# Seven products in place of eight in the MLP's second matrix, for 24 of its 32 row tiles

## The chip, the cores and the metric

One core of a Trainium2 chip runs the whole program. Its engines work side by side and meet only at semaphores: TensorE (PE), VectorE (DVE), ScalarE (ACT), GpSimd (POOL) and SyncE, which issues most transfers. The metric is the device time of one execution in microseconds (us).

## What is computed

A block with latent attention and a state-space mixer, then two layers of a block with sparse and gated attention and an MLP. The change is in the MLP of the two layers:

```python
h = _rms_norm_2(x, g_pre_mlp[l])                       # 512 tokens x 1024
y = jnp.square(jax.nn.relu(h @ w_up[l])) @ w_down[l]   # 1024 -> 4096 -> 1024
x = x + _rms_norm_2(y, g_post_mlp[l])
```

All of it is float32.

## The kernel before

**Products in three parts.** TensorE takes float32 in a rounded form (fp32r). So each operand is split: ScalarE copies it to fp32r (the high part), and another engine subtracts that from the whole (the low part). `product` (L417) then does three matmuls, high x high, high x low, low x high, into one PSUM bank.

**The MLP.** The hidden 4096 are 32 row tiles `f` of 128. An "up" tile is 8 k-tiles x 3 = 24 matmuls of 512 columns (`wide_product`, L1704), weights stationary, tokens moving. The first four up tiles run in halves of 256 tokens (L1915), since the tokens' norm comes in late. Then TensorE does groups `g` of 8 tiles (L1923): the group's up tiles, and then the "down" products with `w_down`, for both halves (512) of the output columns, activations stationary and weights moving, 8 tiles x 4 token tiles x 3 = 96 matmuls of 512 columns a half.

**The other engines.** ScalarE (L2088) makes high parts of the weights (`split_hi`, 1024 elements a tile or pair), four units ahead, and the ReLU out of PSUM (L2097). VectorE makes the low parts of the weights (`split_lo`, L409) and adds each group's outputs to Y (`add_outputs`, L2332). GpSimd (L2390) squares, copies to fp32r and subtracts: `uT_hi` and `uT_lo`. Each engine's list of instructions is written out in the order in which it runs; nothing overtakes.

**Transfers.** SyncE loads the weights into a ring `WR` of 8 slots of 1024 elements, in the order of `units`; a slot is loaded again when the last matmul on its contents is done (`u.free`, L2499).

**Attention's tail.** In `two_pe` the 48 units of scores, transposes of the probabilities and values run as a pipeline over `u` (L1890); then `w_out` is applied in the order `MIX_ORDER` (L1900), one bank for each token tile and half.

Of the kernel before, what the change touches and what calls it, by code (L numbers as in the profile page):

```python
# [51 lines left out]
NSPLIT = J_MLP + 2 * NF  # L52
# [51 lines left out]
class Unit:  # L104
# [16 lines left out]
    "qn_ps score_hi rq_ps rq kn_ps score_lo v1_ps v1 "  # L121
# [35 lines left out]
def build(nc, a, out, first=True, second=True):  # L157
# [16 lines left out]
        "mixT_hi mixT_lo up_ps relu relu_sq down mlp_sum "  # L174
# [3 lines left out]
    with ExitStack() as ctx:  # L178
# [20 lines left out]
        rows, cols = sb("rows", P), sb("cols", ROWS)  # L199
        postg = sb("postg", D)  # L200
# [8 lines left out]
        gf, gx, gate = sb("gf", T, 32), sb("gx", T, NGATE), sb("gate", T, NGATE)  # L209
        ffz, ffm, ffc = (sb(n, SEQ, parts=8) for n in ("ffz", "ffm", "ffc"))  # L210
# [27 lines left out]
        vn, fv = carve(14336, T, 256), carve(15360, T, 512)  # L238
        uT_hi, uT_lo = parts("uT_hi", at_BIG, FG, SEQ), parts("uT_lo", at_BIG + 4 * 4096, FG, SEQ)
# [4 lines left out]
        relu = carve(A0 + 3072, 2, SEQ)  # L244
# [48 lines left out]
        if second:  # L293
            for l in range(DEPTH):
# [62 lines left out]
        def split_of(j):  # L357

            if j < 4:
                return "n1", j, 288  # L360
            if 12 <= j < 16:
                return "n2", j - 12, None
            if j < NPJ:
                return f"t{j}", 0, None
            if j < J_MLP:
                return f"wo{(j - J_OUT) // 4}", (j - J_OUT) % 4, None
            g, i = divmod(j - J_MLP, 2 * FG)
            if i < FG:
                return f"up{FG * g + i}", 0, None
            half, i = divmod(i - FG, FG // 2)  # L370
            return f"dn{half}_{FG * g + 2 * i}", 0, None

        def parts_of(l, j):
# [14 lines left out]
        def split_hi(act, l, j):  # L388
# [6 lines left out]
            elif 20 <= j < NPJ:  # L395
                act.wait_ge(sem.proj, NPJ * l + j - 3)
            elif j >= J_MLP + 4:
                g, i = divmod(j - 4 - J_MLP, 2 * FG)
                if i < FG:
                    act.wait_ge(sem.up_ps, NF * l + FG * g + i + 1)  # L400
                else:
                    act.wait_ge(sem.down, down_count(l, g, (i - FG) // (FG // 2), i % (FG // 2)))
# [8 lines left out]
        def split(pe, l, j):  # L411
# [3 lines left out]
            return hi, lo  # L415

# [551 lines left out]
        def latent_pe(pe):  # L968
# [3 lines left out]
            for h in range(H1):  # L972
# [3 lines left out]
                last.then_inc(sem.qn_ps, 1)  # L976
# [8 lines left out]
            for h in range(H1):  # L985
                pe.wait_ge(sem.score_lo, h + 1)
                nc.tensor.matmul(ps[h][:], wk[:, 256 * h:256 * h + P], ZT[:, 2, :], start=True, stop=True).then_inc(sem.kn_ps, 1)
# [439 lines left out]
        def one_act(act, post_gain):  # L1427
# [167 lines left out]
            for h in range(H1):  # L1595
                act.wait_ge(sem.qn_ps, h + 1)
# [4 lines left out]
            for h in range(H1):  # L1601
                act.wait_ge(sem.kn_ps, h + 1)
# [94 lines left out]
        def two_pe(pe, l):  # L1697
# [192 lines left out]

            for u in range(NU2 + 4):
# [8 lines left out]
            for e, (t, half) in enumerate(MIX_ORDER):  # L1900
                if e == 1:
                    pe.wait_ge(sem.o_sb, NH * (l + 1))
                for k in range(KD):
                    pe.wait_ge(sem.mixT_lo, KD * l + k + 1)
                    w = [v_.rearrange("p (k c) -> p k c", c=512)[:, k % 2, :] for v_ in split(pe, l, J_OUT + 4 * half + k // 2)]
                    x = [v_[:, k, P * t:P * t + P] for v_ in (HT_R, HL_MIX[1])]
                    last = product(ps[mid_bank(t, half)][:], x, w, k == 0, k == KD - 1)
                last.then_inc(sem.out_ps, 1)
# [5 lines left out]

            for step in range(8):  # L1915
# [4 lines left out]
                last = wide_product(ps[up_bank(0) + i], J_MLP + i, HL_MLP, slice(256 * half, 256 * half + 256))  # L1920
                if half:
                    last.then_inc(sem.up_ps, 1)
            for g in range(NG):  # L1923

                for i in range(FG):
                    f = FG * g + i
                    if f < 4:
                        continue
                    if i >= 4:
                        pe.wait_ge(sem.relu, NF * l + f - 3)  # L1930
                    elif g:
                        pe.wait_ge(sem.mlp_sum, mlp_count(l, g - 1, 0))
                    wide_product(ps[up_bank(g) + f % 4], J_MLP + 2 * FG * g + i, HL_MLP).then_inc(sem.up_ps, 1)
# [681 lines left out]
```

## Time and profile before

| | |
|---|---|
| runs | 1729.27 us median (1727.81, 1729.27, 1729.74) |
| profiled execution | 1735.44 us, its span 1733.6 us |
| granted TensorE clock | 0.985 on the mean |
| TensorE busy | 1684.4 us (97%), 8699 matmuls |
| VectorE, ScalarE, GpSimd busy | 823.5 (47%), 599.1 (35%), 518.9 us (30%) |
| the MLP of the first layer | from 674.6 us to about 1034 us of the span |
| that of the second | from 1366.6 us to the end |

Times in the views are microseconds from the span's start; means of one instruction are in nanoseconds. Matmuls are pipelined, and the busy time of one overlaps with the next.

### The profile page before, as it was taken

The numbers are of one execution on the slowest core, as the hardware profiler recorded it, in microseconds if no ns is written. First come the engines' busy times: TensorE is split into PE (matmuls) and PEld (weight loads), VectorE is DVE, ScalarE is ACT, GpSimd is POOL, SyncE is SP. The second block draws the span as 40 slices with busy tenths as digits, with TensorE's granted clock in tenths as the row PEclk, the third lists the DMA queues.
The fourth block names the chain that finished last, engine by engine and source line by source line (L and its number), as shares of the span: only waits on it lengthen the run. The fifth ranks groups of instructions, "written<-read, shape, count | busy, mean of one in ns | idle before, by whom it ended". The sixth has DMA issues, their size and how long they took to land.

```text
span 1733.6 us, 22856 instructions
## 1 busy us (share of the span) xinstructions
PE 1684.4 (97%) x8699; PEld 1269.3 (73%) x8699; DVE 823.5 (47%) x1581; ACT 599.1 (35%) x1210; POOL 518.9 (30%) x594
## 2 busy tenths in 40 slices
PE   7988999999999999999999999999999999999998
PEld 4555457488876678888888888887667888888886
DVE  7999666345337754232323264434774423232324
ACT  3233342242336644322122234233664422222222
POOL 1010001231105654615050623010564461505050
PEclk9999999998999999999999999899999999999999
DMA  6314230135220004332333224422000433232321
GB/s 189 71 25 92 67 110 1 28 111 175 67 87 12 2 1 118 113 96 87 97 98 97 86 56 128 136 62 98 2 2 1 122 110 97 93 90 97 97 85 49
DMA packets 181949, 136.74 MB, mean 79 GB/s; under 512 B 33719, under 2 KB 151218, under 8 KB 181842
## 3 DMA queue, kind: packets, MB, share of 16 engines
q1 hardware_dynamic: 175548, 128.06, 25.0%
q10 hardware_dynamic: 6294, 7.22, 1.9%
q8 instruction: 70, 1.15, 0.3%
q14 instruction: 37, 0.30, 0.1%
HBM read 131.00 MB, written 2.10 MB: 77 GB/s over the span
## 4 chain that ended last, share of the span: by engine, by line
PE 80%; DVE 12%; issue 2%; DMA 2%; POOL 2%; ACT 1%; ACTq 0%; DVEq 0%; POOLq 0%; SPq 0%
PE ps L420 19%; PE ps L419 19%; PE ps L421 19%; PE ps L1855 4%; PE ps L1871 3%; PE ps L1886 3%; PE ps L1055 3%; PE ps L1743 2%; DMA WR<-in_cmp_w_v 1%; PE ps L963 1%; DVE X L558 1%; PE ps L1044 1%; DMA WR<-in_w_up 1%; DVE BIG L1278 1%; PE ps L461 1%
## 5 line engine op out<-in xcount | busy, mean ns | idle before, releaser
L409 DVE TENSOR_TENSOR WR_R<-WR,WH_MLP 128x1024 fp32r<-128x1024 f32 x128 | 159.4, 1245 | 489.6 <-ACT WH_MLP L403 489.6
L421 PE MATMUL ps<-HT_R,WR_R 128*128 128x512 f32 (+1 forms) x832 | 313.8, 377 | 0.0
L403 ACT ACTIVATE WH_MLP<-WR 128x1024 fp32r<-128x1024 f32 x128 | 136.0, 1062 | 502.1 <-PE ps L421 496.9
L2393 POOL TENSOR_TENSOR BIG<-BIG 128x512 f32<-128x512 f32 x64 | 100.3, 1568 | 380.3 <-ACT BIG L2097 380.3
L420 PE MATMUL ps<-HL_MLP,WH_MLP 128*128 128x512 f32 (+1 forms) x576 | 213.8, 371 | 0.0
L419 PE MATMUL ps<-HT_R,WH_MLP 128*128 128x512 f32 (+1 forms) x576 | 213.2, 370 | 0.0
L420 PE MATMUL ps<-WR_R,uT_hi 128*128 128x512 f32 x512 | 203.3, 397 | 0.0
L421 PE MATMUL ps<-WH_MLP,uT_lo 128*128 128x512 f32 x512 | 202.1, 395 | 0.0
L419 PE MATMUL ps<-WH_MLP,uT_hi 128*128 128x512 f32 x512 | 200.1, 391 | 0.0
L421 PEld LDWEIGHTS ps<-HT_R,WR_R 128*128 128x128 f32 x832 | 157.3, 189 | 31.5
L1978 ACT ACTIVATE BIG<-ps 64x512 f32<-64x512 f32 (+3 forms) x124 | 71.8, 580 | 177.2 <-PE ps L421 163.1
L419 PEld LDWEIGHTS ps<-HT_R,WH_MLP 128*128 128x128 f32 x576 | 108.2, 188 | 21.0
L420 PEld LDWEIGHTS ps<-HL_MLP,WH_MLP 128*128 128x128 f32 x576 | 108.4, 188 | 19.9
L2374 POOL TENSOR_SCALAR BIG<-BIG,rg,gate 128x512 f32<-128x512 f32 (+3 forms) x128 | 76.3, 607 | 152.3 <-DVE rg L2261 152.1
L2078 ACT ACTIVATE BIG<-ps,mn 128x512 f32<-128x512 f32 (+1 forms) x192 | 100.3, 528 | 61.5 <-DVE mn L2245 53.9
L2245 DVE CUSTOM_DVE_ANT_0 ps<-ps,tri 128x512 f32<-128x512 f32 (+1 forms) x192 | 93.1, 503 | 58.8 <-PE ps L1855 58.0
L749 PE MATMUL ps<-WR,HT 128*128 128x512 f32 (+1 forms) x256 | 113.5, 593 | 1.4 <-ACT BIG L1532 1.2
L419 PEld LDWEIGHTS ps<-WH_MLP,uT_hi 128*128 128x128 f32 x512 | 96.5, 188 | 23.3
L420 PEld LDWEIGHTS ps<-WR_R,uT_hi 128*128 128x128 f32 x512 | 96.2, 188 | 22.1
L421 PEld LDWEIGHTS ps<-WH_MLP,uT_lo 128*128 128x128 f32 x512 | 96.1, 188 | 20.7
L1855 PE MATMUL ps<-BIG 64*128 64x384 f32 (+7 forms) x384 | 98.2, 480 | 1.6 <-ACT BIG L2078 1.0
L420 PE MATMUL ps<-WR_R,HT_R 128*128 128x512 f32 (+1 forms) x256 | 95.0, 371 | 0.0
(354 smaller groups left out, 2873.1 us busy)
## 6 DMA issues: line engine op xcount, KB each, us to landing
WR<-in_w_up SPq DMA_DIRECT2D x64, 512.0 KB, 4.1
WR<-in_w_down SPq DMA_DIRECT2D x64, 512.0 KB, 3.7
WR<-in_w_in SPq DMA_DIRECT2D x36, 512.0 KB, 5.3
WR<-in_w_out SPq DMA_DIRECT2D x6, 2048.0 KB, 7.9
WR<-in_w_in SPq DMA_DIRECT2D x5, 2048.0 KB, 9.2
WR<-in_cmp_w_k SPq DMA_DIRECT2D x2, 2048.0 KB, 8.3
WR<-in_cmp_w_v SPq DMA_DIRECT2D x2, 2048.0 KB, 8.3
X<-in_x SPq DMA_DIRECT2D x4, 512.0 KB, 5.2
```

The costliest lines, as they stand in the source:

```text
L403: nc.scalar.activation(hi, whole, ACT.Copy).then_inc(sem.w_hi, 1)
L409: nc.vector.tensor_tensor(lo, whole, hi.bitcast(F32), ALU.subtract).then_inc(sem.w_lo, 1)
L419: nc.tensor.matmul(out_, w[0], x[0], start=start, stop=False)
L420: nc.tensor.matmul(out_, w[0], x[1], start=False, stop=False)
L421: return nc.tensor.matmul(out_, w[1], x[0], start=False, stop=stop)
L749: last = nc.tensor.matmul(ps[bank][:, 0:width], HT[:, k, P * m:P * m + P], wv[:, k, 0:width], start=(k == 0), stop=(k == KD - 1))
L1855: nc.tensor.matmul(s_bank(u, o)[:, 0:P * (t + 1)], q_of(kind, h, t), k_of(kind, h, P * (t + 1)), start=True, stop=True).then_inc(sem.s_ps, 1)
L1978: return nc.scalar.activation(dst, src, ACT.Copy, scale=scale)
L2078: nc.scalar.activation(PR[u % 3][:, o, 0:w], s_bank(u, o)[:, 0:w], ACT.Exp, bias=mn[:, i:i + 1], scale=-1.0, accum_out=rs[:, 2 * u + o:2 * ...
L2245: nc.vector.tensor_tensor_reduce(s_bank(u, o)[:, 0:w], s_bank(u, o)[:, 0:w], tri[:, SEQ - w:SEQ], 1.0, 3.0e38, ALU.add, ALU.min, mn[:, i:i ...
L2374: nc.gpsimd.tensor_scalar(PR[u % 3][:, o, 0:w], PR[u % 3][:, o, 0:w], rg[:, u % 3, o:o + 1], g, ALU.mult, ALU.mult)\
L2393: pool_link(nc.gpsimd.tensor_tensor(r, r, r, ALU.mult))
```

## The change

The tiles 0 to 23 go in 12 pairs, two pairs to a round `d` (`NST` = 6 rounds). A pair is the inner dimension's two halves of a 2x2 block product: A (activations) has the halves of 256 tokens as rows and the pair's two tiles as columns; B (weights) has the two tiles as rows and a left and a right block of 256 columns out of the halves of the output. Strassen's scheme in Winograd's form forms four sums on each side (S1 to S4, T1 to T4) and seven products; a product is 2 token tiles x 3 matmuls of 256 columns. A pair needs two such steps ("sweeps"), for the first and the second 256 columns of each half of the output. The seven products of a round's two pairs are accumulated in seven PSUM banks, and VectorE collects them into seven sums Z over the rounds; after the last round eight additions turn the Z into the output. The tiles 24 to 31 stay as they were.

TensorE's order in a round:

```diff
+            whole_up(4)
+            for d in range(NST):
+                strassen_step(d, 0, 0)
+                strassen_step(d, 0, 1)
+                whole_up(4 * d + 5)
+                strassen_step(d, 1, 0)
+                strassen_step(d, 1, 1)
+                for f in range(4 * d + 6, 4 * d + 9):
+                    whole_up(f)
+            for f in range(4 * NST + 5, NF):
+                whole_up(f)
```

A step on TensorE waits for the low parts of the activations (`u_pool`) and of the weight sums (`w_lo`):

```diff
+PRODUCTS = ((A11, B11), (A12, B21), (S4, B22), (A22, T4), (S1, T1), (S2, T2), (S3, T3))
+            def strassen_step(d, sweep, i):
+                n, p = 4 * d + 2 * sweep + i, 2 * d + i
+                pe.wait_ge(sem.u_pool, N_POOL * l + 2 * p + 2)
+                pe.wait_ge(sem.w_lo, NSPLIT * l + step_number(n) + 2)
+                for q, (left, right) in enumerate(PRODUCTS):
+                    if i == 0:
+                        product_bank_free(d, sweep, q)
+                    w = step_right(l, n, right)
+                    for t in range(2):
...
+                        nc.tensor.matmul(out_, x[0], w[0], start=(i == 0 and t == 0), stop=False, skip_group_check=True)
+                        nc.tensor.matmul(out_, x[0], w[1], start=False, stop=False, skip_group_check=True)
+                        last = nc.tensor.matmul(out_, x[1], w[0], start=False, stop=(i == 1), skip_group_check=True)
+                    last.then_inc(sem.prod, 1)
```

The weights of a step: ScalarE `step_hi`, VectorE `step_sums`, `step_lo`, `step_lo_sums`:

```diff
+        def step_hi(act, l, n):
...
+            nc.scalar.activation(H11[i][:], WR[:, u.slot, 0:256], ACT.Copy)
+            nc.scalar.activation(H2[i][:], WR[:, u.slot, 512:1024], ACT.Copy).then_inc(sem.w_hi, 1)
+            act.wait_ge(sem.t_sum, NSTEP * l + n + 1)
+            nc.scalar.activation(WH_MLP[2 * i + 1][:], T_ALL[i], ACT.Copy).then_inc(sem.w_hi, 1)
+        def step_sums(dve, l, n):
...
+            dve_link(nc.vector.tensor_tensor(t[:, 0:512].rearrange("p (b c) -> p b c", c=256), b[:, 1::2, :], b[:, 0:2, :], ALU.subtract))
+            dve_link(nc.vector.tensor_tensor(t[:, 512:768], b[:, 3, :], t[:, 0:256], ALU.subtract))
+            nc.vector.tensor_tensor(t[:, 768:1024], b[:, 2, :], t[:, 512:768], ALU.subtract).then_inc(sem.t_sum, 1)
+        def step_lo(dve, l, n):
...
+            nc.vector.tensor_tensor(WR_R[:, u.slot, 0:256], WR[:, u.slot, 0:256], H11[i][:].bitcast(F32), ALU.subtract)
+            nc.vector.tensor_tensor(WR_R[:, u.slot, 512:1024], WR[:, u.slot, 512:1024], H2[i][:].bitcast(F32), ALU.subtract)\
+                .then_inc(sem.w_lo, 1)
+        def step_lo_sums(dve, l, n):
...
+            nc.vector.tensor_tensor(WH_MLP[2 * i][:], T_ALL[i], WH_MLP[2 * i + 1][:].bitcast(F32), ALU.subtract).then_inc(sem.w_lo, 1)
```

The activations of a pair: ScalarE does ReLU and squares (`unit_done`), `pair_hi` (768 elements) and `pair_hi_sums` (1024); GpSimd does the rest:

```diff
+            for p in range(NPAIR):
+                part = lambda i: U_ALL[p % 3][:, 256 * i:256 * i + 256]
+                pool.wait_ge(sem.u_act, N_ACT * l + 5 * p + 3)
+                pool_link(nc.gpsimd.tensor_tensor(part(S1), A21_[:, p % 2, :], part(A22), ALU.add))
+                pool_link(nc.gpsimd.tensor_tensor(part(S2), part(S1), part(A11), ALU.subtract))
+                nc.gpsimd.tensor_tensor(part(S3), part(A11), A21_[:, p % 2, :], ALU.subtract)
+                nc.gpsimd.tensor_tensor(part(S4), part(A12), part(S2), ALU.subtract).then_inc(sem.u_pool, 1)
+                pool.wait_ge(sem.u_pool, N_POOL * l + 2 * p + 1)
+                for n, cols_ in enumerate((slice(0, 768), slice(768, 1792))):
+                    pool.wait_ge(sem.u_act, N_ACT * l + 5 * p + 4 + n)
+                    last = nc.gpsimd.tensor_tensor(U_LO[p % 3][:, cols_], U_ALL[p % 3][:, cols_], U_HI[p % 3][:, cols_].bitcast(F32),
+                                                   ALU.subtract)
+                last.then_inc(sem.u_pool, 1)
```

The lists of ScalarE and VectorE, of a round:

```diff
+            for d in range(NST):
+                c, b = 4 * d + 4, 4 * d + 3
+                if d == 0:
+                    up_hi(act, l, c)
+                    unit_done(0)
+                    unit_done(1)
+                    pair_hi(0)
+                    step_hi(act, l, 0)
+                    pair_hi_sums(0)
+                    unit_done(2)
+                else:
+                    unit_done(b - 1)
+                    up_hi(act, l, c)
+                    step_hi(act, l, 4 * d)
+                unit_done(b)
+                pair_hi(2 * d + 1)
+                up_hi(act, l, c + 1)
+                step_hi(act, l, 4 * d + 1)
+                pair_hi_sums(2 * d + 1)
+                unit_done(c)
+                step_hi(act, l, 4 * d + 2)
+                up_hi(act, l, c + 2)
+                step_hi(act, l, 4 * d + 3)
+                unit_done(c + 1)
+                if d + 1 < NST:
+                    pair_hi(2 * d + 2)
+                up_hi(act, l, c + 3)
+                if d + 1 < NST:
+                    pair_hi_sums(2 * d + 2)
...
+            for d in range(NST):
+                if d:
+                    collect(d - 1, 1, range(7))
+                up_lo(dve, l, 4 * d + 4)
+                step_sums(dve, l, 4 * d)
+                step_lo(dve, l, 4 * d)
+                step_lo_sums(dve, l, 4 * d)
+                up_lo(dve, l, 4 * d + 5)
+                step_sums(dve, l, 4 * d + 1)
+                step_lo(dve, l, 4 * d + 1)
+                step_lo_sums(dve, l, 4 * d + 1)
+                step_sums(dve, l, 4 * d + 2)
+                collect(d, 0, (0, 1))
+                step_lo(dve, l, 4 * d + 2)
+                collect(d, 0, (2, 3))
+                step_lo_sums(dve, l, 4 * d + 2)
+                collect(d, 0, (4, 5, 6))
+                up_lo(dve, l, 4 * d + 6)
+                step_sums(dve, l, 4 * d + 3)
+                step_lo(dve, l, 4 * d + 3)
+                step_lo_sums(dve, l, 4 * d + 3)
+                up_lo(dve, l, 4 * d + 7)
```

`collect` is one VectorE operation of 512 elements for each product, out of PSUM: a copy in the first round, later an addition to Z.

Outside the MLP, the first 15 matmuls of one output bank of `w_out` move ahead, between the last units of the attention, and two semaphores of the first block are joined into one:

```diff
+            OUT_EARLY = {NU2 + 1: (0, 3), NU2 + 2: (3, 5)}
             for u in range(NU2 + 4):
...
+                if u in OUT_EARLY:
+                    pe.wait_ge(sem.s_exp, NU * (l + 1))
+                    out_product(4, *OUT_EARLY[u])
                 if 0 <= u - 4 < NU2:
                     values(u - 4)
```

The transfer of the second norm's gain (`post_gain`) moves from ahead of the MLP's loop on ScalarE to behind it.

## Rows read from the trace of the kernel before

**Rows 1.** The page, busy time and share of the span of each engine
```profile
PE 1684.4 (97%) x8699; PEld 1269.3 (73%) x8699; DVE 823.5 (47%) x1581; ACT 599.1 (35%) x1210; POOL 518.9 (30%) x594
```
**Rows 2.** The page, the chain that ended last, by engine
```profile
PE 80%; DVE 12%; issue 2%; DMA 2%; POOL 2%; ACT 1%; ACTq 0%; DVEq 0%; POOLq 0%; SPq 0%
```
**Rows 3.** Stretches: length, busy PE, PEld, DVE, ACT, POOL, granted clock, DMA share, GB/s
```profile
605.00:628.00 23.00, 20.45 (x175) 14.32 (x173) 18.56 (x49) 16.07 (x41) 18.85 (x20) 1.00 0.01 1
...
700.00:1011.00 311.00, 311.00 (x1341) 251.75 (x1340) 83.87 (x80) 73.14 (x85) 106.64 (x91) 1.00 0.29 90
```
**Rows 4.** Timeline (start, duration), PE, second matrix: first and last of 37 matmuls
```profile
721.64 0.39 PE L419 MATMUL ps<-WH_MLP,uT_hi 128*128 128x512 f32 x1
...
729.96 0.39 PE L419 MATMUL ps<-WH_MLP,uT_hi 128*128 128x512 f32 x1
```
**Rows 5.** Timeline, PE, first matrix in halves of tokens: first and last of 21 matmuls
```profile
684.01 0.28 PE L421 MATMUL ps<-HT_R,WR_R 128*128 128x256 f32 x1
...
686.36 0.28 PE L420 MATMUL ps<-HL_MLP,WH_MLP 128*128 128x256 f32 x1
```
**Rows 6.** Timeline, ACT: high parts that waited for up tiles 0, 3, 4 and 7
```profile
691.07 1.06 ACT L403 ACTIVATE WH_MLP<-WR 128x1024 fp32r<-128x1024 f32 x1 [6.99 <-PE ps L421]
...
699.51 1.06 ACT L403 ACTIVATE WH_MLP<-WR 128x1024 fp32r<-128x1024 f32 x1 [1.27 <-PE ps L421]
...
705.10 1.06 ACT L403 ACTIVATE WH_MLP<-WR 128x1024 fp32r<-128x1024 f32 x1 [3.12 <-PE ps L421]
...
721.90 1.06 ACT L403 ACTIVATE WH_MLP<-WR 128x1024 fp32r<-128x1024 f32 x1 [4.06 <-PE ps L421]
```
**Rows 7.** Groups by line and shape, 700 to 1010 us (busy us, mean ns | idle before)
```profile
L409 DVE TENSOR_TENSOR WR_R<-WR,WH_MLP 128x1024 fp32r<-128x1024 f32 x56 | 69.5, 1241 | 225.1 <-ACT WH_MLP L403 225.1
L403 ACT ACTIVATE WH_MLP<-WR 128x1024 fp32r<-128x1024 f32 x56 | 59.5, 1062 | 234.4 <-PE ps L421 234.4
...
L2397 POOL TENSOR_TENSOR uT_lo<-BIG,uT_hi 128x512 fp32r<-128x512 f32 x31 | 40.0, 1290 | 2.5
...
L2097 ACT ACTIVATE BIG<-ps 128x512 f32<-128x512 f32 x29 | 16.8, 580 | 0.8 <-POOL uT_lo L2397 0.8
```
**Rows 8.** The same view, whole span, DVE: two inputs in SBUF
```profile
L1097 DVE TENSOR_TENSOR BIG<-BIG 128x512 f32<-128x512 f32 x4 | 2.8, 692 | 0.1
...
L2176 DVE TENSOR_TENSOR BIG<-cmn,BIG 128x256 f32<-128x256 f32 x8 | 3.4, 425 | 0.3
```
**Rows 9.** Timeline, DVE: four copies out of PSUM, merged
```profile
768.52 2.47 DVE L2337 COPY BIG<-ps 128x512 f32<-128x512 f32 x4
```
**Rows 10.** Groups by line and shape, whole span, ACT
```profile
L500 ACT ACTIVATE HT_R<-BIG 128x512 fp32r<-128x512 f32 x32 | 19.5, 630 | 21.3 <-DVE BIG L486 21.3
...
L1978 ACT ACTIVATE BIG<-ps 128x256 f32<-128x256 f32 x32 | 12.0, 378 | 5.7 <-PE ps L1871 4.3 <-PE ps L421 1.4
```
**Rows 11.** Timeline, POOL: one element
```profile
645.85 0.19 POOL L540 TENSOR_TENSOR pms<-pss 128x1 f32<-128x1 f32 x1 [14.11 <-ACT BIG L532]
```
**Rows 12.** Timeline, POOL, the first activations of the MLP
```profile
692.70 1.60 POOL L2393 TENSOR_TENSOR BIG<-BIG 128x512 f32<-128x512 f32 x1 [6.45 <-ACT BIG L2097]
694.36 0.61 POOL L2396 CAST uT_hi<-BIG 128x512 fp32r<-128x512 f32 x1
...
697.32 1.04 POOL L2393 TENSOR_TENSOR BIG<-BIG 128x512 f32<-128x512 f32 x1
698.42 1.49 POOL L2396 CAST uT_hi<-BIG 128x512 fp32r<-128x512 f32 x1
```
**Rows 13.** Timeline, DVE, the same microseconds
```profile
692.17 1.23 DVE L409 TENSOR_TENSOR WR_R<-WR,WH_MLP 128x1024 fp32r<-128x1024 f32 x1 [8.75 <-ACT WH_MLP L403]
...
697.80 1.64 DVE L409 TENSOR_TENSOR WR_R<-WR,WH_MLP 128x1024 fp32r<-128x1024 f32 x1 [1.59 <-ACT WH_MLP L403]
```
**Rows 14.** Timelines, DVE and POOL, end of the attention
```profile
626.00 0.69 DVE L2254 COPY BIG<-ps 128x512 f32<-128x512 f32 x1
...
626.26 1.26 POOL L2380 TENSOR_TENSOR HL_MIX<-BIG,HT_R 128x512 fp32r<-128x512 f32 x1
```

More of the change, by code:

```diff
@@ L238, in build @@
         vn, fv = carve(14336, T, 256), carve(15360, T, 512)
+        U_HI = [parts(f"U_HI{i}", at_BIG + 4 * n, 1792) for i, n in enumerate((0, 1792, 24576))]
+        U_LO = [parts(f"U_LO{i}", at_BIG + 4 * n, 1792) for i, n in enumerate((4096, 5888, 26368))]
+        U_ALL = [BIG[:, n:n + 1792] for n in (4096, 5888, 26368)]
+        A21_ = carve(3584, 2, 256)
         uT_hi, uT_lo = parts("uT_hi", at_BIG, FG, SEQ), parts("uT_lo", at_BIG + 4 * 4096, FG, SEQ)
@@ L415, in split, with up_parts, up_hi @@
             return hi, lo
+        def up_parts(l, f):
+            u = by_name[f"up{f}_{l}"]
+            hi = WH_MLP[f] if f < 4 else UP_HI[f % 2]
+            return u, hi[:], WR_R[:, u.slot, :], WR[:, u.slot, :]
+        def up_hi(act, l, f):
+            u, hi, lo, whole = up_parts(l, f)
+            act.wait_ge(wring[u.slot], u.landed)
+            if f == 5:
+                act.wait_ge(sem.post_y, 8 * (B1 + 2 * l + 1))
+            elif f >= 6:
+                act.wait_ge(sem.up_ps, NF * l + f - 1)
+            nc.scalar.activation(hi, whole, ACT.Copy).then_inc(sem.w_hi, 1)
@@ L1889, in values, with out_product @@
                 last.then_inc(sem.o_ps, 1)
+            def out_product(e, k_from, k_to):
+                t, half = MIX_ORDER[e]
+                for k in range(k_from, k_to):
+                    pe.wait_ge(sem.mixT_lo, KD * l + k + 1)
+                    w = [v_.rearrange("p (k c) -> p k c", c=512)[:, k % 2, :] for v_ in split(pe, l, J_OUT + 4 * half + k // 2)]
+                    x = [v_[:, k, P * t:P * t + P] for v_ in (HT_R, HL_MIX[1])]
+                    last = product(ps[mid_bank(t, half)][:], x, w, k == 0, k == KD - 1)
+                return last
+            OUT_EARLY = {NU2 + 1: (0, 3), NU2 + 2: (3, 5)}
             for u in range(NU2 + 4):
@@ L1902, in two_pe @@
                     pe.wait_ge(sem.o_sb, NH * (l + 1))
[L1903 to L1908, printed above, removed]
+                out_product(e, 5 if e == 4 else 0, KD).then_inc(sem.out_ps, 1)
                 if e == 4:
@@ new lines, in two_pe @@
+            pe.wait_ge(sem.u_act, N_ACT * (l + 1))
+            for t in range(T):
+                for i in range(FG):
+                    w = down_right(i, 1)
+                    x = [v[:, i, P * t:P * t + P] for v in (uT_hi, uT_lo)]
+                    last = product(ps[in_bank(t, 1)][:], x, w, i == 0, i == FG - 1)
+                last.then_inc(sem.down, 1)
+                if l + 1 < DEPTH and t >= 2:
+                    norm_transpose(pe, v + 2, t - 2)
+        BANKS = (0, 1, 2, 3, 5, 6, 7, 4)
@@ new lines, in two_dve @@
+            for d in range(NST):
+                if d:
[19 more added lines that the diff above has]
+                up_lo(dve, l, 4 * d + 7)
@@ L2295, in two_dve @@
+            for i in range(8):
+                down_lo(dve, l, i)
+                if i == 5:
+                    add_outputs(dve, l, 0, range(T))
             w = w0 + 1
@@ L2507, in _ @@
                         dst = dst[:, c:c + h * n].rearrange("p (h n) -> p h n", h=h)
+                    elif where is not None and where[0] == "s":
+                        dst = dst[:, where[1]:where[1] + 512].rearrange("p (h c) -> p h c", h=2)
                     elif where is not None:
```

358 lines of the change are left out of this document (238 added, 120 removed).

## The prediction

> **What bounds the kernel now.** I read the page's shares of busy time first: TensorE is busy for 97% of the span and no other engine for half of it [rows 1]. The chain that ended last says the same, 80% of it is TensorE [rows 2]. Then the stretches: in the MLP TensorE is busy for 311.00 of 311.00 us, while VectorE works 84, ScalarE 73 and GpSimd 107 us; the last groups of the attention ahead of it leave TensorE idle for 2.55 of 23 us [rows 3]. So in the MLP every column that TensorE doesn't stream is time, until another engine is late. A busy row of TensorE is no price, since matmuls overlap: one of 512 columns shows 0.39 us and the next starts 0.23 us later. I take start to start.
>
> **TensorE's saving.** In the second matrix 36 starts of 512 columns take 729.96 - 721.64 = 8.32 us, 0.2311 us each [rows 4]. Half-width products exist already, the first four tiles of the first matrix by halves of tokens: 20 starts of 256 columns take 2.35 us, 0.1175 us each, so cutting a matmul in two costs 2% and each load of weights still hides [rows 5]. Per pair of tiles the change takes away 2 tiles x 4 token tiles x 2 halves x 3 = 48 matmuls (11.09 us) and adds 2 sweeps x 7 products x 2 token tiles x 3 = 84 of half width (9.87 us). That is 1.22 us a pair, and 29.3 us for 12 pairs in each of two layers: 1.7%.
>
> **What the other engines get, by volume.** A round (`d`) is four up tiles, two pairs, four steps. An up tile takes 5.60 us (705.10 to 721.90 for three, [rows 6]), a step 42 x 0.1175 = 4.94, so a round takes TensorE 42.2 us. VectorE: an operation of 1024 elements 1.24 us, of 512 0.69, of 256 0.43 [rows 7, 8]; back to back about 0.08 less, the four copies in 2.47 us being 0.62 each [rows 9]. Four low parts of up tiles, four steps of (512, 256, 256 sums; 256, 512 and 1024 low parts), 14 collects of 512: some 28 us. ScalarE at 1.06 for 1024, 0.58 for 512 out of PSUM, 0.63 in SBUF and 0.38 for 256 [rows 7, 10]: 22 us. GpSimd: 512 elements with two inputs take 1.29 us [rows 7], one element 0.19 [rows 11]; on that line 256 take 0.74, 768 1.83, 1024 2.4, so a pair costs 4 x 0.74 + 1.83 + 2.4 = 7.2 and a round 14.4 us. Everything fits in 42.2. Transfers fit too: each ring slot is refilled eight units, one round, ahead, with the same bytes, and DMA's share is 0.29 [rows 3]. By volume alone the change would win.
>
> **But VectorE and GpSimd take turns.** GpSimd's squaring (512 elements) takes 1.04 us alone and 1.60 when VectorE's subtraction of two SBUF tiles still runs: 692.17 + 1.23 = 693.40, and 694.30 less 1.04 is 693.26. The other way round, a subtraction issued at 697.80 during GpSimd's squaring takes 1.64 instead of 1.23, and the cast behind it 1.49, which alone is 0.61 [rows 12, 13]. One waits for the whole of the other, the waiting one goes next, and hand-over wins back some 0.15 us. A VectorE operation fed from PSUM does not do it: GpSimd's 1.26 at 626.26 is its price alone, with a copy out of PSUM beside it [rows 14]. The Trainium skill says the same (SBUF — State Buffer, "Who interferes with whom": the shared pair "is an exclusive lock, not a bandwidth split", held against a VectorE instruction with two SBUF inputs); the trace agrees by these rows. Before, there was one such subtraction in 5.6 us; now sums and low parts of the weights on VectorE and sums and low parts of the activations on GpSimd fall in the same few microseconds.
>
> **The chain that is late.** The second step of a round, S01 (tiles 4d+2, 4d+3), needs the low parts of its activations (GpSimd) and of its weight sums (VectorE). Ahead of it on TensorE stand only the tile 4d+4 and the step S00: 5.60 + 4.94 = 10.54 us after the end of tile 4d+3. Put that end at 0. ScalarE learns of it at 0.26 (721.90 against 721.64 [rows 4, 6]), but ScalarE and VectorE do not look ahead: their lists are fixed, and the list of this round began only when tile 4d+2 ended at -5.60. From there: ReLU and squares to -4.0, high part of tile 4d+4 to -3.0, its low part to -1.8, three linked sums of step 4d to -0.2, their high part on ScalarE to 0.86. Then ScalarE: ReLU 0.77 to 1.35, square to 2.0, high part of 768 to 2.9, high part of tile 4d+5 to 3.9, of the step's blocks to 4.7, and it waits for VectorE's sums. GpSimd has begun S1 at 2.1, S2 at 2.9, S3 at 3.6. VectorE wants the low part of 4d+5 at 3.9, gets it at 4.2 to 5.4; GpSimd's S4 5.3 to 6.0; first sum 5.9 to 6.55; GpSimd's 768 from 6.4 to 8.25; the second and third sum to 9.0. ScalarE: high part of these sums to 10.1, then `pair_hi_sums` (1024) to 11.05. VectorE's last low part 10.1 to 11.35 holds GpSimd's 1024, which ends at 13.6. TensorE starts S01 3.1 us late. Without turns the same list gives 11.2, 0.7 us late. Behind TensorE's late step all other waits have room again (S10's weights are there some 4 us early, S11's 2 us), so the stall doesn't feed on itself: it repeats in each of five rounds per layer.
>
> The first round is tighter. The first four up tiles end 2.81 us apart, at 691.07 to 699.51 for ScalarE, tile 4 at 705.10 [rows 6]; S01 could start at 709.8. ScalarE takes tile 2 only behind step 0 and `pair_hi_sums(0)`, at 699.6; tile 3 to 702.1; high part of pair 1 to 703.0, of tile 5 to 704.0; VectorE and GpSimd then alternate (low part to 705.2, sums to 708.1), high part of the sums to 709.2, of the activation sums to 710.2, GpSimd's 1024 and VectorE's 1024 behind each other to 714.5: 4.7 us late, 1.2 without turns.
>
> **Small parts.** The eight additions of 1024 after the last round (9.8 us on VectorE) lie under six whole up tiles (33.6 us), of whose low parts the second is due some 17 us in and ready at about the same time: 0 to 1 us a layer, taken as 0. `OUT_EARLY` puts 15 matmuls (3.5 us) between the last attention groups and takes them from behind; TensorE's idle 2.55 us [rows 3] lie before the first of the two places for the most part, so I count 0, bounds 0 to 2 us gained a layer. The semaphore renamed in the first block and `post_gain` moved behind the loops (its transfer has the second half of the last products, over 20 us, to land in) cost 0.
>
> **Sum.** -29.3 + 10 x 3.1 + 2 x 4.7 = +11 us. The profiled execution took 1735.44 us (span 1733.6), so about 1746.5 there; it lies 6.2 us above the median of the runs, and the difference goes to the median: 1729.27 + 11 = 1740.
>
> **Rivals.**
> 1. The chain has room that I don't see (hand-overs cheaper, the 1024 and 768 operations shorter than my line, no turns where operations are short). With 0.7 and 1.2 us of stall it is 9.4 us against 29.3: 1709. The rows for turns are clear, which speaks against it; but the forecast changes sign if the mean stall is 2.4 us and not 3.4, one microsecond in a chain of 13.6, which speaks for it. Chance 0.30, from 1706 to 1727.
> 2. The forecast: late at S01 in every round, gain more than eaten. It needs a mean stall over 2.4 us. Chance 0.50, own range 1730 to 1752.
> 3. Turns bite elsewhere too: each of the short sums waits for a whole GpSimd operation and each GpSimd sum for a VectorE one, the stall goes to 5 us a round (12 x 5 - 29.3 = +31, 1760), or S00 or S10 become late as well. For it: three engines with fixed lists, each waiting in order. Against it: 4 us of room at S10. Chance 0.15.
> 4. The saving isn't there: half-width products with activations as weights, seven products with a semaphore each, run slower than 0.1175. At 48 x 0.2311 / 84 = 0.132 us a start nothing is saved, and with the stalls it is 1769. The half-width rows are of the other operand order, which is all that speaks for it; at full width both orders go at 0.231 to 0.233. Chance 0.05.
>
> **Numbers.** About 0.2% (3.5 us) is what a measurement can tell from no change: 1725.8 to 1732.7. That zone gets 0.12 from the edges of rivals 1 and 2; faster 0.31, slower 0.57. Range 1709 to 1761: it takes in the case without turns and stops at the third rival's price.
>
> **What would show it.** Starts 0.117 to 0.118 apart within a step confirm the saving. TensorE idle 3 us ahead of the second step of each round, 4 to 5 in the first, released by GpSimd's low part in U_LO (behind `pair_hi_sums`), and GpSimd's operations of 256 elements showing over 1 us next to VectorE's sums, confirm the chain. TensorE's busy share of the MLP near 93% and an MLP some 5 us longer per layer follow. No idle at S01 would prove me wrong, idle at other steps the third rival, starts above 0.13 the fourth.

## The result: 43 us slower, not 11

| | before | after |
|---|---|---|
| runs, median | 1729.51 us (4 runs, 1727.81 to 1737.68) | 1772.67 us (4 runs, 1768.08 to 1780.14) |
| ratio | 1 | 1.0244 [1.0196, 1.0292] |
| profiled execution, its span | 1735.44, 1733.6 us | 1772.09, 1770.0 us |
| matmuls | 8699 | 9563 |
| first MLP: first matmul to the transposes after it | 674.58 to 1034.40, 359.8 us | 672.05 to 1053.27, 381.2 us |

The sign was forecast; the size was not, and 1772.67 lies above the range (1709 to 1761). In the profiles the MLP grew by 21.4 us in the first layer and by 21.6 in the second (367.0 us before and 388.6 after, to the end of the span), 43.0 together; the medians differ by 43.2. The spans of the two profiles differ by 36.4 only. The rest is outside the MLPs, where the execution of before had the lower granted clock: 0.98 up to the first MLP and 0.96 between the two, against 0.99 and 0.97.

The page of after, engines and the chain that ended last (they answer to [rows 1, 2]):

```profile
PE 1672.6 (94%) x9563; PEld 1303.7 (74%) x9563; DVE 1114.7 (63%) x1955; ACT 713.6 (40%) x1426; POOL 564.8 (32%) x594
...
PE 73%; DVE 15%; ACT 4%; issue 3%; POOL 3%; DMA 2%; ACTq 0%; POOLq 0%; DVEq 0%; SPq 0%
```

TensorE is busy 11.8 us less in a span 36.4 us longer, so it stands idle for 48.2 us more. The list of what TensorE waited for in the first MLP (total, times, longest) names the waits; before, the same list held one wait of 0.5 us, behind the MLP.

```profile
PE ps L2115 <- POOL U_LO L2708: 14.8, 5, 3.0
PE ps L2115 <- DVE WH_MLP L548: 5.0, 1, 5.0
PE ps L563 <- DVE WR_R L485: 3.4, 1, 3.4
PE ps L563 <- DVE WR_R L506: 0.9, 1, 0.9
PE ps L605 <- DVE BIG L590: 0.2, 1, 0.2
```

The first two lines are S01, the second step of a round, late in all six rounds, for 19.8 us. The next two come after the rounds, among the last up tiles and the full-width tiles: 4.3 us that the prediction put at nothing. The two layers have 2 x (19.8 + 4.3) = 48.2 us of such waits.

Four stretches of after (length, busy PE, PEld, DVE, ACT, POOL, granted clock, DMA share, GB/s): the whole MLP, a first sweep with its wait, a later first sweep, and the piece of the latter right behind its wait. The MLP answers to [rows 3].

```profile
672.00:1053.00 381.00, 356.70 (x2088) 315.87 (x2088) 260.51 (x305) 151.96 (x233) 153.18 (x122) 0.97 0.30 88
752.50:765.70 13.20, 10.24 (x85) 10.01 (x84) 12.96 (x16) 6.05 (x9) 5.15 (x3) 1.00 0.26 79
798.10:812.80 14.70, 11.74 (x85) 11.52 (x84) 14.03 (x17) 6.04 (x9) 5.14 (x3) 0.88 0.24 71
807.10:810.40 3.30, 3.30 (x17) 3.30 (x17) 2.97 (x7) 2.00 (x2) 0.00 (x0) 0.50 0.00 0
```

Both sweeps wait 2.96 us. The first keeps clock 1.00 and takes 13.2 us. The second falls to 0.50 (1.2 GHz instead of 2.4) a microsecond behind the wait and takes 14.7. TensorE's timeline (start, duration, what it waited for) shows the same matmuls in both clocks:

```profile
760.64 0.39 PE L2115 MATMUL ps<-H,U_HI 128*128 128x256 f32 x1 [2.96 <-POOL U_LO L2708]
...
806.23 0.39 PE L2115 MATMUL ps<-H,U_HI 128*128 128x256 f32 x1 [2.96 <-POOL U_LO L2708]
...
806.81 0.28 PE L2116 MATMUL ps<-WR_R,U_HI 128*128 128x256 f32 x1
806.93 0.29 PE L2117 MATMUL ps<-H,U_LO 128*128 128x256 f32 x1
...
807.45 0.41 PE L2117 MATMUL ps<-H,U_LO 128*128 128x256 f32 x1
807.66 0.41 PE L2115 MATMUL ps<-H,U_HI 128*128 128x256 f32 x1
```

806.81 to 806.93 is 0.12 us; 807.45 to 807.66 is 0.21. So a wait of 3 us costs 3 us, and in 7 of the 10 later rounds of the two layers 1.5 us again, because the steps behind it run at half clock for some 3 us.

**The late chain is the one forecast.** Engines on the same round, VectorE, GpSimd, then ScalarE:

```profile
796.34 1.68 DVE L485 TENSOR_TENSOR WR_R<-WR,UP_HI 128x1024 fp32r<-128x1024 f32 x1 [1.75 <-ACT UP_HI L479]
797.94 1.22 DVE L531 TENSOR_TENSOR BIG<-WR 128x512 f32<-128x512 f32 x1
799.20 1.96 DVE L532 TENSOR_TENSOR BIG<-WR,BIG 128x256 f32<-128x256 f32 x1
801.19 0.42 DVE L533 TENSOR_TENSOR BIG<-WR,BIG 128x256 f32<-128x256 f32 x1
```

```profile
796.19 0.74 POOL L2703 TENSOR_TENSOR BIG<-BIG 128x256 f32<-128x256 f32 x1
796.89 1.72 POOL L2704 TENSOR_TENSOR BIG<-BIG 128x256 f32<-128x256 f32 x1
798.69 2.19 POOL L2708 TENSOR_TENSOR U_LO<-BIG,U_HI 128x768 fp32r<-128x768 f32 x1
803.74 2.44 POOL L2708 TENSOR_TENSOR U_LO<-BIG,U_HI 128x1024 fp32r<-128x1024 f32 x1 [2.86 <-ACT U_HI L2325]
```

```profile
801.65 1.06 ACT L523 ACTIVATE WH_MLP<-BIG 128x1024 fp32r<-128x1024 f32 x1 [4.51 <-DVE BIG L533]
802.62 1.04 ACT L2325 ACTIVATE U_HI<-BIG 128x1024 fp32r<-128x1024 f32 x1
```

A sum of 256 elements that takes 0.42 us alone (801.19) takes 1.96 (799.20), until GpSimd's 768 is through (798.69 + 2.19 = 800.88). GpSimd's fourth sum takes 1.72 instead of 0.74, behind VectorE's subtraction. ScalarE stands still for 4.51 us until VectorE's last sum is ready, then makes the high part for which GpSimd's 1024 waits, and this ends at 806.18; S01 starts at 806.23.

### The profile page after: what moved, and what is told of

Read it like the earlier page. It is cut to its first block, busy times and chain, and to the rows that moved or that the text cites. A ratio compares the mean times of both kernels' runs of the same rounds, so it can differ in the third digit from the quotient of the medians.

```text
span 1770.0 us, 25358 instructions
## 1 busy us (share of the span) xinstructions
PE 1672.6 (94%) x9563; PEld 1303.7 (74%) x9563; DVE 1114.7 (63%) x1955; ACT 713.6 (40%) x1426; POOL 564.8 (32%) x594
## 4 chain that ended last, share of the span: by engine, by line
PE 73%; DVE 15%; ACT 4%; issue 3%; POOL 3%; DMA 2%; ACTq 0%; POOLq 0%; DVEq 0%; SPq 0%
PE ps L563 13%; PE ps L564 13%; PE ps L565 12%; PE ps L2115 4%; PE ps L2117 4%; PE ps L2116 4%; PE ps L1999 4%; PE ps L2015 3%; PE ps L2030 3%; PE ps L1199 3%; POOL U_LO L2708 1%; PE ps L1887 1%; DMA WR<-in_cmp_w_v 1%; PE ps L605 1%; DVE BIG L2594 1%
## 5 line engine op out<-in xcount | busy, mean ns | idle before, releaser
L563 PE MATMUL ps<-HT_R,UP_HI 128*128 128x512 f32 x448 | 178.7, 399 | 6.7 <-DVE WR_R L485 6.7
L564 PE MATMUL ps<-HL_MLP,UP_HI 128*128 128x512 f32 x448 | 178.0, 397 | 0.0
L485 DVE TENSOR_TENSOR WR_R<-WR,UP_HI 128x1024 fp32r<-128x1024 f32 x56 | 82.7, 1477 | 144.0 <-ACT UP_HI L479 143.9
L2115 PE MATMUL ps<-H,U_HI 128*128 128x256 f32 x288 | 86.8, 301 | 39.5 <-POOL U_LO L2708 29.6
L2708 POOL TENSOR_TENSOR U_LO<-BIG,U_HI 128x768 fp32r<-128x768 f32 (+1 forms) x48 | 107.8, 2258 | 31.3 <-ACT U_HI L2325 29.4
L2115 PE MATMUL ps<-WH_MLP,U_HI 128*128 128x256 f32 x384 | 110.8, 289 | 0.0
L2116 PE MATMUL ps<-WH_MLP,U_HI 128*128 128x256 f32 x384 | 110.4, 288 | 0.0
L2117 PE MATMUL ps<-WH_MLP,U_LO 128*128 128x256 f32 x384 | 110.1, 287 | 0.0
L563 PEld LDWEIGHTS ps<-HT_R,UP_HI 128*128 128x128 f32 x448 | 85.0, 190 | 26.6 <-issue 7.5
L2567 DVE TENSOR_TENSOR BIG<-ps,BIG 128x512 f32<-128x512 f32 x140 | 93.4, 686 | 14.8 <-PE ps L2117 13.0
L564 PEld LDWEIGHTS ps<-HL_MLP,UP_HI 128*128 128x128 f32 x448 | 85.0, 190 | 18.6
```

The costliest lines, as they stand in the source:

```text
L563: nc.tensor.matmul(out_, w[0], x[0], start=start, stop=False)
L564: nc.tensor.matmul(out_, w[0], x[1], start=False, stop=False)
L2115: nc.tensor.matmul(out_, x[0], w[0], start=(i == 0 and t == 0), stop=False, skip_group_check=True)
L2116: nc.tensor.matmul(out_, x[0], w[1], start=False, stop=False, skip_group_check=True)
L2117: last = nc.tensor.matmul(out_, x[1], w[0], start=False, stop=(i == 1), skip_group_check=True)
L2567: nc.vector.tensor_tensor(z, src, z, ALU.add).then_inc(sem.z_sum, 1)
```

## Experiments

Each kernel is the changed one unless it says otherwise. The ratio is that to the kernel before on the same chip; where there is none, there was one run and its profile.

**rounds.** From the second round on, ScalarE and VectorE split the first steps of the round ahead of its new up tiles, and the order of loads follows. The core of the edit:

```diff
                 else:
+                    step_hi(act, l, 4 * d)
                     unit_done(b - 1)
                     up_hi(act, l, c)
-                    step_hi(act, l, 4 * d)
+                    step_hi(act, l, 4 * d + 1)
                 unit_done(b)
                 pair_hi(2 * d + 1)
...
+                else:
+                    pair_hi_sums(2 * d + 1)
+                    unit_done(c)
+                    up_hi(act, l, c + 1)
```

> The changed kernel with its lists for ScalarE and VectorE in another order in rounds 1 to 5: the weights of both first steps are split ahead of the up tiles 4d+2 and 4d+3, the activation sums of pair 2d+1 directly behind its first high part. Nothing is taken out. Theory A (fixed lists plus turns make S01 late; the half clock follows that idle time): TensorE's idle 2.96 us at S01 is gone in ten rounds, the half-clock stretches of these rounds with it; they stay only in the first round and ahead of up tile 29. Span about 1770 - 30 - 9 = 1731 us, near the kernel before. Rival B (the half clock comes from the denser work of all engines, not from idle time): stretches at 0.5 of 3.4 us stay in most rounds, span about 1740. Rival C (S01 is bound by the volume of GpSimd and VectorE taking turns, not by the order): 1.5 us or more of idle time stay at S01, span about 1750.

Median 1729.64 us of 10 runs, ratio 0.9975 [0.9944, 1.0007], span 1731.3. Five rounds, timeline cut into one stretch:

```profile
750.00:955.00 205.00, 205.00 (x1293) 184.70 (x1292) 143.28 (x200) 95.30 (x140) 76.86 (x60) 1.00 0.34 101
```

TensorE is busy in all 205 us at clock 1.00, each pair of steps takes 10.01 to 10.03 us, and the waits left are the first round's 5.0 and the end's 3.4 and 0.9. The same products on the same engines in another order: 1.0244 - 0.9975 = 2.7% of the time, 46 us, is gone. The profile of after accounts for 42.5 of it: the ten later first sweeps took 29.6 us of idle time and 12.9 us beyond it over 10.03 each. The intervals leave room for the rest. The other engines do the same work as in after, TensorE has no gap, and the clock stays at 1.00: dense work alone doesn't bring the half clock.

**rounds_first_end.** The same, and the order mended in the first round and at the end, where the eight additions now stand one or two between low parts:

```diff
             plus(2, 5)
+            up_lo(dve, l, F_PLAIN + 6)
             dve_link(plus(6, 5))
-            up_lo(dve, l, F_PLAIN + 5)
             dve_link(plus(3, 6))
+            up_lo(dve, l, F_PLAIN + 7)
```

> As rounds, and also: in the first round step 1's weights ahead of up tile 5's, and at the end the eight additions of the sums Z spread out between the low parts of up tiles 28 to 31, and the low part of dn6 ahead of the four additions of outputs. Theory A: idle at S01 in the first round falls from 4.96 to about 1.5 us (GpSimd's two pairs in a row bind it), idle ahead of tile 29 (3.36) and in the last products (0.93) is gone with their half-clock stretches. Then per layer the saving of 12.8 us on TensorE and 2.5 us at the end of the attention are left: span about 1733.6 - 2 x (12.8 + 2.5 - 3) = 1709 us. Rival B: the half clock stays in the rounds, about 1718. Rival D (the saving is eaten by something that I have not seen): no faster than the kernel before.

Median 1713.06 us of 10 runs, ratio 0.9886 [0.9854, 0.9917]. The end's waits are gone; its up tiles, 146 matmuls:

```profile
952.50:986.00 33.50, 33.50 (x146) 27.04 (x145) 22.34 (x15) 8.70 (x11) 24.33 (x15) 1.00 0.31 95
```

The first round still waits 3.6 us where I expected 1.5. GpSimd's own rows tell why: the 768 and the 1024 of pair 0 take 5.54 us by turns with VectorE (the two take 1.83 + 2.4 = 4.2 in the prediction), and the sums of pair 1 begin behind them, at 709.59; its last low part ends at 718.49, just ahead of S01.

```profile
704.10 5.54 POOL L2717 TENSOR_TENSOR U_LO<-BIG,U_HI 128x768 fp32r<-128x768 f32 x2
709.59 0.92 POOL L2710 TENSOR_TENSOR BIG<-BIG 128x256 f32<-128x256 f32 x1
```

TensorE's waits in this kernel's first MLP are this one line:

```profile
PE ps L2115 <- POOL U_LO L2717: 3.6, 1, 3.6
```

**end_only.** The edit of the end alone.

> The changed kernel with only its end in another order: the eight additions of Z spread between the low parts of up tiles 28 to 31, dn6's low part ahead of the additions of outputs. Theory A (additions with two SBUF inputs take turns with GpSimd's last tiles, 1.92 us each, and tile 29's low part stands behind five of them): idle 3.36 + 0.93 us a layer gone, with a half-clock stretch worth 1.4 us: span 1770 - 2 x 5.7 = 1759 us. Rival E: the wait moves to tile 30 or 31 (same additions, same turns), span within 3 us of 1770.

1760.07 us in one run, and a span 12.0 us shorter than that of after. The up tiles of the end take 33.53 us instead of 38.42, the full-width second-matrix tiles 38.83 instead of 40.16: 6.2 us a layer. After, the up tiles of that stretch:

```profile
968.20:1006.60 38.40, 35.04 (x146) 27.98 (x146) 22.55 (x15) 8.69 (x11) 22.93 (x15) 0.96 0.26 83
```

VectorE's timeline in it:

```profile
976.76 9.63 DVE L2594 TENSOR_TENSOR BIG<-BIG 128x1024 f32<-128x1024 f32 x5
986.42 1.95 DVE L485 TENSOR_TENSOR WR_R<-WR,UP_HI 128x1024 fp32r<-128x1024 f32 x1
```

Five additions take 9.63 us, 1.93 each, where a VectorE operation of 1024 elements takes 1.23 alone: they go by turns with GpSimd's squares, casts and low parts. The low part for the next up tile comes behind all five and ends at 988.37; TensorE has waited 3.36 us and then runs at half clock.

**memset_pool.** GpSimd's four sums of a pair and its subtraction of 768 elements are left out; constants are written in their place. Everything else, ScalarE's and VectorE's lists among it, stays.

```diff
-                pool_link(nc.gpsimd.tensor_tensor(part(S1), A21_[:, p % 2, :], part(A22), ALU.add))
-                pool_link(nc.gpsimd.tensor_tensor(part(S2), part(S1), part(A11), ALU.subtract))
-                nc.gpsimd.tensor_tensor(part(S3), part(A11), A21_[:, p % 2, :], ALU.subtract)
-                nc.gpsimd.tensor_tensor(part(S4), part(A12), part(S2), ALU.subtract).then_inc(sem.u_pool, 1)
+                nc.gpsimd.memset(U_ALL[p % 3][:, 768:1792], 0.5).then_inc(sem.u_pool, 1)
```

> The changed kernel with its lists as they are; GpSimd's four sums of a pair are left out (one memset of the same 1024 elements stands there) and so is its first subtraction of 768 elements (a memset). Its last subtraction, of 1024, stays. So GpSimd reads SBUF only behind the chain's end, and VectorE's sums find nobody to take turns with; the order of the lists is unchanged. Theory A (turns make 2.3 of the 2.96 us): idle at S01 0.7 to 0.9 us in ten rounds, 1.2 in the first; VectorE's second sum L532 0.43 us instead of 1.96; hardly a half-clock stretch in the rounds; the end (3.36 us) unchanged. Span about 1770 - 10 x 2.2 - 2 x 3.7 - 12 = 1729 us. Rival C (the fixed order alone makes the wait, or GpSimd's own time): idle at S01 stays above 2.5 us.

1717.26 us. Here VectorE's lists haven't moved, only GpSimd's part beside them is gone. VectorE's timeline, ScalarE's and GpSimd's behind it, and TensorE's:

```profile
788.55 0.42 DVE L532 TENSOR_TENSOR BIG<-WR,BIG 128x256 f32<-128x256 f32 x1
```

```profile
789.47 1.06 ACT L523 ACTIVATE WH_MLP<-BIG 128x1024 fp32r<-128x1024 f32 x1 [1.98 <-DVE BIG L533]
```

```profile
791.56 2.49 POOL L2708 TENSOR_TENSOR U_LO<-BIG,U_HI 128x1024 fp32r<-128x1024 f32 x1 [4.92 <-ACT U_HI L2325]
```

```profile
750.99 0.39 PE L2115 MATMUL ps<-H,U_HI 128*128 128x256 f32 x1 [0.48 <-POOL U_LO L2708]
```

The sum that took 1.96 us takes 0.42, the wait at S01 is 0.47 to 0.48 instead of 2.96 in the ten later rounds, and no round falls to half clock. Take the same round in both, counted from the start of S00 (798.12 in after, 788.47 here): ScalarE's high part of the sums starts 3.53 us in there and 1.00 us in here, 2.53 earlier, and GpSimd's 1024 moves by the same 2.53. VectorE's three operations ahead account for all of it: the low part L485 takes 1.68 there and 1.22 here, L531 1.22 and 0.69, L532 1.96 and 0.42. GpSimd's own work has no part in it: its 1024 takes 2.44 there and 2.49 here, and in after it stood idle for 2.86 us ahead of that. So 2.5 of the 2.96 us are turns; the list without turns had given 0.7. The span, 1715.4 us, is some 14 below what I expected: less idle time in the first rounds (0.36 us, not 1.2), none of the half clock there, and 6 us outside the MLPs.

**ladder.** The order of rounds_first_end, with a wait of chosen length put ahead of S01, a different one in each round: GpSimd writes a small constant tile one to eight times before it lets TensorE go. Nothing is left out.

```diff
+                if d and not sweep and i:
+                    pe.wait_ge(sem.idled, (NST - 1) * l + d)
...
+                if p % 2 and p > 1:
+                    pool.wait_ge(sem.prod, step_done(l, 2 * (p - 1)))
+                    for m in range(PAUSES[l][p // 2] - 1):
+                        pool_link(nc.gpsimd.memset(hidr[:], 0.0))
+                    nc.gpsimd.memset(hidr[:], 0.0).then_inc(sem.idled, 1)
```

> rounds_first_end with a pause of known length for TensorE ahead of S01 in each round after the first (TensorE waits until GpSimd has made 1 to 8 memsets that start when S00 ends): about 0.9, 1.4, 1.9, 2.4, 2.9 us in the first layer, 3.4, 3.9, 4.4, 2.4, 2.9 us in the second. Theory A (TensorE's idle time alone brings the half clock): none behind the short pauses, a stretch of 3.4 us behind most of 2.9 us and more; other engines have no part in it. Rival B (dense work of all engines): no half-clock stretch in any round, since without pauses there was none. Nothing is left out of the computation.

1751.88 us. The pauses came out at:

| TensorE's idle ahead of S01 | 0.73 | 1.32 | 1.90 | 2.48 | 2.49 | 3.06 | 3.06 | 3.65 | 4.23 | 4.81 |
|---|---|---|---|---|---|---|---|---|---|---|
| half clock behind it | no | no | no | no | no | yes | yes | yes | yes | yes |
| the two steps take | 10.97 | 11.55 | 12.14 | 12.72 | 12.72 | 14.81 | 14.81 | 15.38 | 15.98 | 17.64 |
| less 10.03 and the idle | 0.21 | 0.20 | 0.21 | 0.21 | 0.20 | 1.72 | 1.72 | 1.70 | 1.72 | 2.80 |

Two neighbours of the table on TensorE's timeline, and the stretches behind them (columns as above):

```profile
889.54 0.35 PE L2118 MATMUL ps<-H,U_HI 128*128 128x256 f32 x1 [2.48 <-POOL hidr L2727]
...
935.21 0.36 PE L2118 MATMUL ps<-H,U_HI 128*128 128x256 f32 x1 [3.06 <-POOL hidr L2727]
```

```profile
889.60:893.00 3.40, 3.40 (x29) 3.40 (x30) 2.45 (x5) 1.22 (x2) 0.00 (x0) 1.00 0.21 65
...
936.90:940.00 3.10, 3.10 (x16) 3.10 (x16) 2.93 (x5) 0.00 (x0) 1.28 (x1) 0.51 0.02 5
```

In 3.4 us at full clock 29 matmuls run, in 3.1 us at half clock 16. Up to 2.49 us of idle time costs itself and 0.2 (an idle time is counted from the end of the last matmul, whose last 0.16 us would have overlapped with the next one); from 3.06 on it costs 1.5 us more or above. The waits of 3.58 us in the two first rounds were followed by half clock too. The waits of 2.96 us in after lie between: half clock in 7 of 10 rounds, and again in 7 of 10 in end_only (2.93 to 2.97 us). The ladder's rounds differ in the length of the pause alone, in which GpSimd writes its constants; in after it wrote none, and the half clock came all the same. So TensorE's idle time is the cause.

**before_halves.** The kernel before, its second-matrix products cut into halves of columns, nothing else: what a start costs in this operand order.

```diff
-                            last = product(ps[down_bank(g, half) + t][:], x, w, i == 0, i == FG - 1)
+                            for c in (0, 256):
+                                out_ = ps[down_bank(g, half) + t][:, c:c + 256]
+                                y = [v[:, c:c + 256] for v in w]
```

> The kernel before, each matmul of the second matrix with 512 columns cut into two of 256 (last half of the last group excepted), activations stationary, no Strassen. It measures the price of a half-width start in this operand order. The changed kernel's steps ran at 0.1194 us a start, not 0.1175. Theory A (half width with this order costs 0.1194, whatever sums stand behind it): 0.119 to 0.120 here, and an MLP longer by 2 x 0.1194 - 0.2311 = 0.008 us for each of 672 matmuls a layer, span +10 to +11 us. Rival G (the extra 0.002 us come from the product's semaphores and waits): 0.1175 here, span +5 us.

1730.02 us. First and last of 40 starts in a row:

```profile
730.09 0.28 PE L1960 MATMUL ps<-WR_R,uT_hi 128*128 128x256 f32 x1
...
734.84 0.28 PE L1961 MATMUL ps<-WH_MLP,uT_lo 128*128 128x256 f32 x1
```

(734.84 - 730.09) / 40 = 0.1188 us, against 0.1175 in [rows 5]. The change's own steps go at 10.03 / 84 = 0.1194. So two thirds of the excess over 0.1175 come with this operand order; what the last 0.0006 us come from was not measured. The first MLP came out 4.4 us longer (364.2), and the second 4.2. That the whole was no slower than before goes with 14 us less outside the MLPs in that execution (granted clock 0.99 up to the first and between the two, against 0.98 and 0.96 in before), so one run says nothing on the sum.

**before_early.** The kernel before with `OUT_EARLY` alone (the lines as in the diff above).

> The kernel before, with only the 15 matmuls of one bank of w_out moved ahead between the last attention units. The MLP of the changed kernel began 2.5 us earlier in the first layer. Theory A: this move alone gives it, 2 x 2.5 = 5 us, ratio 0.997. Rival F: the earlier start comes from the loads (two more free ring slots or the gain's transfer moved), then this kernel is within 1 us of the one before.

Median 1737.63 us of 10 runs, ratio 1.0034 [1.0005, 1.0062]: no gain, a loss of a few us if anything. In its profile the first MLP began at 675.9 us and that of before at 674.58, both with a granted clock of 0.98 up to there; that of after began at 672.05 with 0.99. So the earlier start that I had seen went with the clock, not with this move.

**rfe_no_early.** rounds_first_end without `OUT_EARLY`.

```diff
-            OUT_EARLY = {NU2 + 1: (0, 3), NU2 + 2: (3, 5)}
+            OUT_EARLY = {}
...
-                out_product(e, 5 if e == 4 else 0, KD).then_inc(sem.out_ps, 1)
+                out_product(e, 0, KD).then_inc(sem.out_ps, 1)
```

> rounds_first_end with the 15 early matmuls of w_out put back behind the attention. Theory A (the early matmuls bring a half-clock stretch with them at the attention's end, 630 and 1340 us, and save nothing: before_early was at 1.0034): 0 to 5 us faster than rounds_first_end, ratio to the kernel before 0.984 to 0.989. Rival H (they save 1 to 2 us a layer and before_early was unlucky in its clock): ratio 0.990 or more. Either way faster than both kernels.

Median 1708.30 us of 6 runs, ratio 0.9878 [0.9841, 0.9914], beside 0.9886 [0.9854, 0.9917] with it: not told apart. Both beat the kernel before, by 1.1 and 1.2%, with intervals that end below 1. Of these 20 us the profiles show 15 in the MLPs: 8.1 and 6.9 us shorter than before in rounds_first_end, 7.0 and 7.9 here. The cheaper products' 2 x 12.7 us are there, less some 11.5 us that the waits of the two first rounds and what follows them still cost, which leaves 14 of these 15. The other 5 us lie within the intervals and are not explained.

## Why the prediction was right or wrong

Three terms of the sum failed: it charged TensorE's waits by their length alone (a wait of 2.96 us cost 3.2 or 4.7), it put the end of the MLP at nothing (6.2 us a layer), and it took the saving 1.9 us a layer too large. The waits themselves, their places and their cause were forecast rightly. The layer in terms of the sum (us, first layer of the profile of after):

| | predicted | measured |
|---|---|---|
| twelve pairs of tiles, products alone | -14.65 | 12 x (10.03 - 11.09) = -12.7 |
| S01 late, idle time | 5 x 3.1 + 4.7 = 20.2 | 4.96 + 3 x 2.96 + 2 x 2.97 = 19.8 |
| beyond S01's idle time | not in the sum | 28.25 - 19.8 = 8.5: half clock 7.2, lost overlap 6 x 0.21 = 1.3 |
| the end: up tiles and full-width tiles | 0 (bound 1) | 4.9 + 1.3 = 6.2 |
| together | +5.5 | +21.8; the MLP grew by 21.4 |

28.25 is what the six first sweeps (17.78, 13.23, 14.73, 14.73, 13.24, 14.72 us) took beyond 10.03 each; 0.21 is what the ladder's pauses at full clock cost beyond their length. Twice 21.8 is 43.6 beside 43.2 measured.

- **What bounds the kernel** was right, and stayed so only where TensorE was fed: in `rounds` 205 us of 205.
- **The saving** was right in kind and 1.9 us a layer too large. The term that failed is the price 0.1175, taken from half-width products of the other operand order; with this order `before_halves` shows 0.1188 and the steps themselves 0.1194. Rival 4, which put the starts above 0.132, is out.
- **The late chain** held by its times and its cause. The forecast's 3.1 and 4.7 us stand beside 2.96 and 4.96, in every round, and what TensorE waited for was GpSimd's low part in five rounds. In the first it was VectorE's low part (L548): the two ends that I had put behind each other fell in the other order. `memset_pool` shows turns to be the cause (0.48 us left, and the 2.53 us found in VectorE's three operations), `rounds` shows that the order of the lists makes them matter. Rival 1 (room in the chain) is out. That the stall doesn't feed on itself was right too: pairs of steps behind it take 10.03 us. (The words that the forecast quotes from the Trainium skill stand in another section of the same page, "SBUF: two separate sides"; the section that it names has the rule on two SBUF inputs.)
- **The half clock** failed by omission, and with 7.2 us a layer it is the largest miss; the lost overlap of 1.3 us stands beside it. The sum charged a wait of 3.1 us at 3.1 us. The forecast spoke of waits of 3.1 and 4.7 us, and by the ladder both are of the length that costs 1.5 us and more beyond themselves. The profile of before had stretches below full clock outside the MLP (0.96 on the mean between the two MLPs), and I priced none. The Trainium skill warns of this (TensorE: Matmul & The Clock Gate, "HAM oscillation — how this bites in real kernels": idle gaps in a loop can return the clock to its lower level each time, so that the cost is paid again in every turn); the ladder agrees behind its pauses of 3.06 us and more, and the rounds of after do in 7 of 10.
- **"Small parts"** failed at the eight additions: 9.8 us on VectorE were costed alone, though the same text had shown that two inputs in SBUF go by turns with GpSimd, which works on the activations of those up tiles. With turns five take 9.63 us, the second low part isn't ready in time, and the end costs 6.2 us a layer (4.3 of them idle time), not 0 to 1. This is rival 3's mechanism, "turns bite elsewhere too", at a place that it did not name; it named S00 and S10, and neither was late.
- **`OUT_EARLY` at 0** was slightly kind, if it was off: 1.0034 [1.0005, 1.0062] on the kernel before, and no difference between `rounds_first_end` and `rfe_no_early`.
- **The numbers.** With 8.5 + 6.2 + 1.9 us a layer added and 0.4 less of idle time, 11 becomes 11 + 2 x 16.2 = 43. The range failed because its upper end was the price of longer waits alone; none of its cases had a wait that costs more than its length.

Three things stay open. Which of the waits of 2.96 us are followed by half clock was not settled; 3 of 10 are not. What makes the steps' starts 0.1194 us apart and not 0.1188 was not measured. And `rounds_first_end` still waits 3.6 us in each first round; no order that ends it was tried.

## What to carry to other kernels

Before an algorithm with fewer matmuls is put in, write out the lists of the engines that prepare its operands, with each operation charged at its price beside the engine that it takes turns with, and do so for the additions at the end as well as for the loop. Charge an idle gap of TensorE by its length plus what the clock takes behind it, and keep the gaps short. When a change loses with its products cheaper, reorder before giving it up: here the same work was 2.4% slower in one order and 1.1% faster in another.

## What the runs showed of the hardware

- TensorE's granted clock after one gap between dense rounds of the MLP: 1.00 after 0.73 to 2.49 us, half after 3.06 to 4.96 us, either after 2.96. The half clock cost about 1.5 us behind most gaps, and 2.4 to 2.7 behind some of 3.58 us and more (2.6 behind 4.96 us in the first layer of after, 1.3 behind 4.95 in the second).
- Shorter gaps did not always spare the clock. At the end of the attention TensorE waited for 0.99 and then 0.95 us; in after it was busy for 1.36 of 3.3 us there, and 3.4 us at half clock followed. In before the same two waits were followed by clock 1.00.

```profile
616.00:619.30 3.30, 1.36 (x12) 0.71 (x10) 2.34 (x5) 1.48 (x6) 3.30 (x4) 1.00 0.00 0
619.30:622.70 3.40, 3.40 (x23) 2.74 (x24) 2.34 (x6) 2.13 (x4) 3.40 (x6) 0.50 0.00 0
```

- A VectorE sum of 256 elements took 0.42 us alone and 1.96 beside one GpSimd operation of 768, so a short operation is held up by what is left of the other engine's, however short it is itself.
- Five VectorE additions of 1024 beside GpSimd took 1.93 us each, where an operation of 1024 takes 1.23 alone, and GpSimd's cast of 512 took 1.49 to 1.50 beside them, 0.61 alone in [rows 12].
- Matmuls of 256 columns start 0.1175 us apart in the first matrix and 0.1188 to 0.1194 in the second, more than half of the 0.2311 of 512 columns; the saving of seven products for eight was 9.6% of their time (10.03 against 11.09), not 12.5%.
